# Routing a mixture of experts in four batches between the output projections

## The chip, the cores and the metric

One core of one Trainium2 chip runs the whole program. The metric is device time in microseconds of one execution, from the start to the end of the program on that core. Lower is better. TensorE (PE) multiplies matrices, VectorE (DVE), ScalarE (ACT) and GpSimd (POOL) work on tiles in on-chip memory, SyncE (SP) issues most transfers. Each engine runs its own instructions in order and waits on semaphores.

## What is computed

One layer of a decoder trunk for 1024 prompt rows and 8 sample rows, 1024 wide: a mixer of linear attention and sliding-window attention, an output projection with a gated residual, a norm, and then a mixture of 16 experts of which each row uses two. The part that the change touches:

```python
def moe(h, router_w, router_b, wg, wu, wd):
    x = h.reshape(-1, D)
    scores = sigmoid(x @ router_w)                       # (rows, 16)
    sel = scores + router_b
    group_score = top_k(sel.reshape(n, 4, 4), 2)[0].sum(-1)
    gmask = one_hot(argmax(group_score), 4)              # best group of four experts
    masked = where(repeat(gmask, 4), sel, -inf)
    _, top_idx = top_k(masked, 2)                        # two experts in it
    top_w = take_along_axis(scores, top_idx); top_w /= top_w.sum(-1, keepdims=True)
    hid = silu(einsum('nd,edf->nef', x, wg)) * einsum('nd,edf->nef', x, wu)
    y = einsum('nef,efd->nd', hid * gate[:, :, None], wd)
```

## The kernel before

The program is written as five instruction streams with hand-placed semaphores, in stages that end with a barrier of all five engines (`stage_end`, L494 to L497: each engine drains, counts up, and waits for the other four). Stage 4 is the one of the change: output projection, norm, routing. Stage 5 is the experts.

Rows are worked on in nine tiles: eight of 128 prompt rows and one of the 8 sample rows, which is the last (`PT` = 8 prompt tiles, `NT` = 9). In stage 4 TensorE runs `project(t)` (L1793: 8 k-steps by two halves of 512 columns, 16 matmuls in 32 records) and `route(t)` (L1804: eight transposes of the normed tile, a wait for ScalarE's copy of them, eight logit products), in the order project 0, project 1, route 0, project 2, route 1, ..., project 8, route 7, route 8 (L1819 to L1823). VectorE follows each projection with gate, residual and norm (L1323 to L1341), between whose steps ScalarE squares, sums and takes the root (L960 to L968); SP loads the x tile for it and stores the normed rows to memory (`h2_rows`, L643 to L652).

When all nine routes are done, ScalarE takes the exponential of all logits (L970, L972), and VectorE works on all 9 x 16 = 144 columns at once: scores, best group, two best experts (L1349 to L1382). TensorE counts with two products against a strict triangle and against ones (L1825, L1826): the rank of each row inside its tile for its expert, and the counts per tile. VectorE adds up the tiles (L1389), turns counts into the number of half tiles of each expert and their starts (L1393 to L1398), and gives each row two slots in one packed list (L1400 to L1408). `route_ok` tells the other engines. GpSimd then writes the row numbers into `slot_token` with 18 indirect scatters, two per tile (L725 to L730), and waits for all of them. VectorE meanwhile writes the table of starts `etab` (L1410 to L1412), the weights of the combination (L1415 to L1420) and the low halves of three quarters of the first expert's weights (`split_piece`, L1422 to L1429). SP has issued those loads behind the last norm (L653 to L655), then a store of zeros to `slot_token` (L658) and the load of the first expert's third matrix.

Behind the barrier GpSimd runs one `gather` per tile of an expert (L737): a load of 128 row numbers from `slot_token`, then an indirect gather of those rows of `h2_rows`. TensorE, ScalarE and VectorE run the experts in loops over `etab`. An expert has one full tile of 128 slots and then half tiles of 64. The results go to `slot_rows`, and a last stage gathers two of them per row by `ids`.

Of the kernel before, what the change touches and what calls it, by code (L numbers as in the profile page):

```python
# [27 lines left out]
U32 = mybir.dt.uint32  # L28
# [4 lines left out]
P = 128  # L33
# [26 lines left out]
X_LOADS = ((NT + 1) // 2, NT // 2)  # L60
GN = S + P - 1
# [17 lines left out]
for _name, _w in (("ident", P), ("ones", P), ("cum_mid", P), ("cum", P), ("cum_rest", P), ("strict", P),  # L79
                  ("blk", HA * DV), ("oh", GN), ("ohs", CK + 1), ("seq8", NB), ("diag8", NB * HD),  # L80
                  ("eprio", NE), ("gprio", NG), ("thr", HALVES), ("before", NE * NE), ("srows", 1), ("tokid", NT),
# [45 lines left out]
def build(nc, x_prompt, x_sample, state_gla, cache_win_k, cache_win_v, c_prompt, c_sample, w_ada, b_ada, norm1_g,  # L127
# [23 lines left out]
    slot_token = nc.dram_tensor("slot_token", [SLOTS + 2 * P, 1], U32, kind="Internal").ap()  # L151
    slot_rows = nc.dram_tensor("slot_rows", [SLOTS, D], F32, kind="Internal").ap()

    with ExitStack() as ctx:
# [5 lines left out]
        ids = ctx.enter_context(nc.sbuf_tensor("ids", [P, 2 * NT + NT + 2], U32))  # L160
# [215 lines left out]
        sqj2 = V(a1, D); a1 += D  # L376

# [16 lines left out]
        zero_i = R(SLOTS // P + 2)  # L394
# [46 lines left out]
        so_ps = sem("so_ps"); osq_ok = sem("osq_ok"); ossq_ok = sem("ossq_ok"); ostd_ok = sem("ostd_ok")  # L441
# [8 lines left out]
        ohb_ok = sem("ohb_ok"); qb_ps = sem("qb_ps"); slog_ok = sem("slog_ok"); sprod = sem("sprod")  # L450
        selfd_ok = sem("selfd_ok"); slT_ps = sem("slT_ps"); smax_ok = sem("smax_ok"); sexp_ok = sem("sexp_ok")
        sp_ok = sem("sp_ok"); spT_ps = sem("spT_ps"); spT_ok = sem("spT_ok"); sov_ps = sem("sov_ps")
        smix_ok = sem("smix_ok"); smask_ok = sem("smask_ok")
# [3 lines left out]
        rexp2 = sem("rexp2"); both_ok = sem("both_ok"); rank_ps = sem("rank_ps"); route_ok = sem("route_ok")  # L457
# [43 lines left out]
        def _(sp):  # L501
# [142 lines left out]
            for t in range(NT):  # L644
                if t >= 2:
                    sp.wait_ge(res_ok, t - 1)
                sp.dma_start(xr[t % 2][0:rows_of(t)], xp[t * P:(t + 1) * P] if t < PT else xs).then_inc(x_in[t % 2], 16)
                if t >= 1:
                    sp.wait_ge(norm_ok, NT + t)
                    sp.dma_start(h2_rows[(t - 1) * P:t * P], h2[(t - 1) % 2]).then_inc(h2_out[(t - 1) % 2], 16)  # L650
            sp.wait_ge(norm_ok, 2 * NT)
            sp.dma_start(h2_rows[S:TOK], h2[PT % 2][0:NB]).then_inc(h2_out[PT % 2], 16)  # L652
# [4 lines left out]
            sp.wait_ge(zero_ok, 2)  # L657
            sp.dma_start(slot_token.rearrange("(p n) a -> p (n a)", p=P), zero_i.bitcast(U32)).then_inc(st_zero, 16)  # L658
# [21 lines left out]
            sp.wait_ge(route_ok, 2)  # L680
# [12 lines left out]
        def _(pool):  # L693
# [23 lines left out]
            stage_end(pool, 3)  # L717
            bc.done(nc.gpsimd.partition_broadcast(bcG1, modrow(G1)[32:33]), wait=False)
# [6 lines left out]
            for t in range(NT):  # L725
                n = rows_of(t)
                for j in range(2):
                    nc.gpsimd.indirect_dma_start(  # L728
                        slot_token, bass.IndirectOffsetOnAxis(ap=ids[0:n, 2 * t + j:2 * t + j + 1], axis=0),
                        ids[0:n, 2 * NT + t:2 * NT + t + 1], None).then_inc(st_out, 16)  # L730
# [4 lines left out]
            pool.wait_ge(route_ok, 2)  # L735

            def gather(t, u):  # L737
                pool.dma_start(gidx[:], slot_token[bass.ds(u * HR, P), :]).then_inc(gi_in, 16)
# [29 lines left out]
        def _(act):  # L768
# [191 lines left out]
            for t in range(NT):  # L960
# [5 lines left out]
                if t >= 1:  # L966
                    act.wait_ge(lr_ps, t)
# [76 lines left out]
        def _(dve):  # L1044
# [278 lines left out]
            for t in range(NT):  # L1323
                n = rows_of(t)
                dve.wait_ge(op_ps, t + 1)
                if t == 0:
                    dve.wait_ge(bc_ok, 6)
# [651 lines left out]
```

## Time and profile before

| | us |
|---|---|
| median of three runs (lowest, highest) | 1471.78 (1471.03, 1472.57) |
| the profiled execution, whole time | 1473.51 |
| its span, first to last instruction | 1471.9 |
| TensorE busy | 1194.3 (81%) |
| VectorE busy | 564.3 (38%) |
| ScalarE busy | 465.3 (32%) |
| GpSimd busy | 96.2 (7%) |
| mean granted TensorE clock, share of full speed | 0.897 |

Stage 4 lies between 771.2 and 986.4 us of the span. How to read the rows further down: a row of the chain or of a timeline begins with its start and its length in us; L with a number is a line of the kernel; out<-in are the program's names with the shapes (128x512 is partitions by elements); x32 is the number of instructions in the row; in square brackets stands how long the engine had been idle and who ended it. An engine's name with a q (POOLq) is its sequencer. One f32 matmul leaves two records.

### The profile page before, as it was taken

How to read it: one execution, taken by the hardware profiler on the slowest of the kernel's cores; microseconds unless marked ns; L12 is line 12 of the kernel's file. 1: busy time of each engine (PE TensorE's matmuls, PEld its weight loads, DVE VectorE, ACT ScalarE, POOL GpSimd, SP SyncE). 2: the span in 40 equal slices, each digit the busy share in tenths (PEclk: the TensorE clock that was granted, in tenths of full speed). 3: DMA queues.
4: the chain of work that ended last, by engine and by line, in shares of the span. 5: the costliest groups of instructions: out<-in, count | busy, mean ns of one | idle time of the engine just before them, and what ended most of it. 6: DMA issues, size and time to landing. Idle time of an engine off the chain costs nothing.

```text
span 1471.9 us, 18511 instructions
## 1 busy us (share of the span) xinstructions
PE 1194.3 (81%) x6985; PEld 640.1 (43%) x6986; DVE 564.3 (38%) x851; ACT 465.3 (32%) x777; POOL 96.2 (7%) x110
## 2 busy tenths in 40 slices
PE   4995985975999999999689999305999999999910
PEld 1232553653556565565344444102455545555400
DVE  3256014325222323324802222522553544445347
ACT  0123013413333333334001111203544544445333
POOL 0000000000000000000000000051000001000022
PEclk9997996985999999999589999656999999999965
DMA  6974001004530312107722111416998888978445
GB/s 231 344 284 154 1 1 43 1 9 132 212 92 8 89 41 60 46 12 197 207 85 86 53 52 41 158 52 221 345 364 278 296 281 317 326 272 301 148 170 189
DMA packets 127706, 228.13 MB, mean 155 GB/s; under 512 B 10588, under 2 KB 49145, under 8 KB 127516
## 3 DMA queue, kind: packets, MB, share of 16 engines
q1 hardware_dynamic: 114748, 195.98, 39.1%
q0 software_dynamic: 7168, 21.06, 4.2%
q10 hardware_dynamic: 5728, 10.23, 1.8%
q8 instruction: 43, 0.70, 0.2%
q14 instruction: 19, 0.16, 0.0%
HBM read 193.45 MB, written 33.79 MB: 154 GB/s over the span
## 4 chain that ended last, share of the span: by engine, by line
PE 63%; DVE 7%; ACT 5%; DMA 4%; issue 2%; SPq 2%; POOL 2%; POOLq 0%; ACTq 0%; DVEq 0%
PE banks L1801 9%; PE banks L1864 8%; PE banks L1536 4%; PE banks L1537 4%; PE banks L1538 4%; PE banks L1837 4%; PE banks L1838 4%; PE banks L1839 4%; PE banks L1874 3%; PE banks L1733 2%; PE banks L1888 2%; PE banks L1652 2%; PE banks L1781 2%; PE banks L1845 2%; POOL slot_token L728 1%
## 5 line engine op out<-in xcount | busy, mean ns | idle before, releaser
L1426 DVE SCALAR_TENSOR_TENSOR arena<-arena 128x2048 f16<-128x2048 f32 x64 | 143.8, 2288 | 126.9 <-ACT arena L977 126.9
L1536 PE MATMUL banks<-arena 128*128 128x384 f16 (+4 forms) x536 | 176.2, 329 | 9.3 <-DVE arena L1105 9.3
L1537 PE MATMUL banks<-arena 128*128 128x384 f16 (+4 forms) x536 | 175.9, 328 | 0.0
L1538 PE MATMUL banks<-arena 128*128 128x384 f16 (+4 forms) x536 | 175.7, 328 | 0.0
L977 ACT ACTIVATE arena<-arena 128x2048 f16<-128x2048 f32 x64 | 118.9, 1911 | 72.4 <-DMA arena<-in_moe_w_up_dram 45.0
L1801 PE MATMUL banks<-arena 128*128 128x512 f32 (+1 forms) x288 | 130.6, 614 | 0.3 <-DVEq L496 0.3
L1864 PE MATMUL banks<-arena 128*128 128x512 f32 x256 | 113.9, 598 | 12.5 <-ACT arena L1000 12.5
L1837 PE MATMUL banks<-arena 128*128 128x512 f16 x256 | 98.3, 384 | 2.6 <-DVE arena L1438 2.6
L1838 PE MATMUL banks<-arena 128*128 128x512 f16 x256 | 98.2, 384 | 0.0
L1839 PE MATMUL banks<-arena 128*128 128x512 f16 x256 | 98.0, 383 | 0.0
L1511 PE MATMUL banks<-arena 128*33 128x512 f32 x192 | 85.7, 604 | 0.5 <-ACT arena L777 0.5
L1801 PEld LDWEIGHTS banks<-arena 128*128 128x128 f32 (+1 forms) x288 | 52.2, 184 | 72.3 <-issue 71.8
L1864 PEld LDWEIGHTS banks<-arena 128*128 128x128 f32 x256 | 47.3, 190 | 69.7 <-issue 62.3
L908 ACT ACTIVATE arena<-arena 128x128 f32<-128x128 f32 (+7 forms) x96 | 53.4, 557 | 70.9 <-DVE arena L1235 70.9
L1536 PEld LDWEIGHTS banks<-arena 128*128 128x128 f16 (+1 forms) x536 | 51.8, 97 | 48.7 <-issue 15.3
L1845 PE MATMUL banks<-arena 128*128 128x128 f32 x192 | 26.2, 281 | 56.5 <-DMA arena<-h_rows,gidx 56.5
L1538 PEld LDWEIGHTS banks<-arena 128*128 128x128 f16 (+1 forms) x536 | 52.0, 97 | 36.4 <-issue 1.0
L1235 DVE CUSTOM_DVE_ANT_0 arena<-banks,arena 128x128 f32<-128x128 f32 (+7 forms) x96 | 43.7, 492 | 62.5 <-PE banks L1652 59.3
L1537 PEld LDWEIGHTS banks<-arena 128*128 128x128 f16 (+1 forms) x536 | 51.9, 97 | 34.2 <-issue 0.8
L1260 DVE COPY arena<-banks 128x256 f32<-128x256 f32 (+3 forms) x72 | 27.3, 407 | 74.3 <-PE banks L1733 74.0
L1438 DVE TENSOR_TENSOR arena<-banks,arena 128x1024 f16<-128x1024 f32 x24 | 29.4, 1225 | 63.0 <-ACT arena L991 63.0
L1733 PE MATMUL banks<-arena 128*128 128x128 f32 (+3 forms) x276 | 43.4, 277 | 11.3 <-ACT arena L914 6.7
(337 smaller groups left out, 1562.9 us busy)
## 6 DMA issues: line engine op xcount, KB each, us to landing
arena<-in_moe_w_gate_dram SPq DMA_DIRECT2D x32, 1024.0 KB, 5.4
arena<-in_moe_w_up_dram SPq DMA_DIRECT2D x32, 1024.0 KB, 8.7
arena<-in_moe_w_down_dram SPq DMA_DIRECT2D x16, 2048.0 KB, 11.7
arena<-in_w_ada_dram SPq DMA_DIRECT2D x12, 2048.0 KB
arena<-in_w_in_dram SPq DMA_DIRECT2D x18, 512.0 KB, 5.7
arena<-in_x_prompt_dram SPq DMA_DIRECT2D x16, 512.0 KB, 4.8
slot_rows<-arena SPq DMA_DIRECT2D x2, 4096.0 KB, 20.1
slot_rows<-arena ACTq DMA_DIRECT2D x32, 256.0 KB, 7.2
```

Of the source, the lines that this page charges most:

```text
L977: A(w_hi[s][p // 2][:, (p % 2) * PIECE:(p % 2 + 1) * PIECE], stage[p], ACT.Copy, scale=WS).then_inc(phi_ok, 1)
L1426: v.scalar_tensor_tensor(out=w_lo[s][p // 2][:, part], in0=stage[p], scalar=WS, in1=w_hi[s][p // 2][:, part], op0=ALU.mult, op1=ALU.subtra ...
L1511: last = mm(bank(4 + j % 3, 512, 33), csT[:, k], wa[j % 3][:, k], start=(k == 0), stop=(k == KC - 1))
L1536: mm(out, hTh[:, k, tok], wh(k), start=(first and k == ks[0]), stop=False)
L1537: mm(out, hTh[:, k, tok], wl(k), start=False, stop=False)
L1538: done = mm(out, hTl[:, k, tok], wh(k), start=False, stop=(last and k == ks[-1]))
L1733: last = tr(out[0:w, j * P:(j + 1) * P], p[:, o:o + w], ident)
L1801: last = mm(bank(b + h, 512, n), mixT[:, k, t * P:t * P + n], w[:, 512 * h:512 * h + 512], start=(k == 0), stop=(k == KC - 1))
L1837: mm(out, xh[:, k], wh(k), start=(k == 0), stop=False)
L1838: mm(out, xh[:, k], wl(k), start=False, stop=False)
L1839: done = mm(out, xl[:, k], wh(k), start=False, stop=(k == ks[-1]))
L1864: last = mm(bank(5 + h), hidT[:, k * P:(k + 1) * P], wD[s][:, k * D + h * 512:k * D + h * 512 + 512], start=(k == 0), stop=(k == 3))
```

## The change

The samples' tile is projected first instead of last, in four column groups of TensorE: product k goes to the 32 output partitions from 32*(k % 4) on, so that each group sums two of the eight k-steps; ScalarE copies the four partial sums, and a product with `sel8` (ones at rows r, r + 32, r + 64, r + 96) adds them. Routing is cut in four batches: the samples, tiles 0 to 2, 3 to 5, 6 and 7. Each batch is gated (`gates`, ScalarE), chosen (`choose`, VectorE), counted (`count`, TensorE), and placed (`place`, VectorE) between the projections and norms of later tiles. `run` holds the running counts, so that a rank is final when its batch is placed. An expert now owns a fixed region of 1152 slot numbers in `slot_token`, so the scatters of a batch need no expert starts; GpSimd issues them batch by batch. The packed slots that the combination needs are made once at the end, behind the expert table. The zeros of `slot_token` (now 145 columns) are cleared and stored at the start of the stage.

```diff
+ORDER = (PT,) + tuple(range(PT))
+BATCHES = ((PT, NT), (0, 3), (3, 6), (6, PT))
+CAP = 1152
...
 SP
             sp.dma_start(rw, router_w.rearrange("(k p) n -> p k n", p=P)).then_inc(vec_in, 16)
+            sp.wait_ge(zero_ok, 2)
+            sp.dma_start(slot_token[0:NE * CAP + P].rearrange("(p n) a -> p (n a)", p=P), zero_i.bitcast(U32)).then_inc(st_zero, 16)
...
-            sp.wait_ge(zero_ok, 2)
-            sp.dma_start(slot_token.rearrange("(p n) a -> p (n a)", p=P), zero_i.bitcast(U32)).then_inc(st_zero, 16)
...
 GpSimd
+            nc.gpsimd.memset(zero_i, 0.0).then_inc(zero_ok, 1)
             bc.done(nc.gpsimd.partition_broadcast(bcG1, modrow(G1)[32:33]), wait=False)
...
-            nc.gpsimd.memset(zero_i, 0.0).then_inc(zero_ok, 1)
             pool.wait_ge(st_zero, 16)
-            pool.wait_ge(route_ok, 1)
-            for t in range(NT):
-                n = rows_of(t)
-                for j in range(2):
+            for b, (t0, t1) in enumerate(BATCHES):
+                pool.wait_ge(slots_ok, b + 1)
+                for t in range(t0, t1):
+                    n = rows_of(t)
+                    for j in range(2):
...
-                gather(start, start + e)
+                gather(start, e * CAP)
                 with pool.If(end - start - 1):
-                    with pool.Fori(start + 1, end) as t:
-                        gather(t, t + e + 1)
+                    with pool.Fori(1, end - start) as j:
+                        gather(start + j, e * CAP + j * HR + HR)
...
 ScalarE
+            act.wait_ge(part_ps, 1)
+            A(opart, banks[:, 2048:2048 + D], ACT.Copy).then_inc(part_ok, 1)
+            def gates(b):
+                t0, t1 = BATCHES[b]
+                act.wait_ge(lr_ps, t1 + 1 if t1 < NT else 1)
...
+                A(sco[0:rows_of(t0), t0 * NE:t1 * NE], src, ACT.Exp, scale=-1.0).then_inc(rexp2, 1)
+            for s, t in enumerate(ORDER):
...
                 A(rs[0:n, t:t + 1], ss[0:n, t:t + 1], ACT.Sqrt, scale=1.0 / D, bias=eps[0:n]).then_inc(rms_ok, 1)
+                if t == PT - 1:
+                    A(V(o_stat, 1), C("one"), ACT.Exp)
...
+                for b, (t0, t1) in enumerate(BATCHES):
+                    if t == t1 - 1:
+                        gates(b)
...
 VectorE
+            lk.done(v.memset(banks[:, 2048:2048 + D], 0.0), wait=False)
+            lk.done(v.tensor_tensor(sel8, ident[:, 0:NB], ident[:, 32:32 + NB], ALU.add))
+            lk.done(v.tensor_tensor(sel8, sel8, ident[:, 64:64 + NB], ALU.add))
+            v.tensor_tensor(sel8, sel8, ident[:, 96:96 + NB], ALU.add).then_inc(sel8_ok, 1)
...
+            def choose(b):
+                dve.wait_ge(rexp2, b + 1)
...
+            def place(b):
+                dve.wait_ge(rank_ps, b + 1)
+                for t in range(t0, t1):
+                    lk.done(v.tensor_tensor(rank[:, c], banks[:, r:r + NE], run, ALU.add))
+                    lk.done(v.tensor_tensor(run, run, banks[:, r + 64:r + 64 + NE], ALU.add))
+                lk.done(v.tensor_tensor(v3(E_(tB)), v3(E_(rank)), C("ecap").unsqueeze(1).broadcast_to([P, m, NE]), ALU.add))
+                for j, one in enumerate((one1, one2)):
+                    lk.done(v.tensor_tensor(E_(tA), E_(tB), E_(one), ALU.mult))
+                    lk.done(v.tensor_reduce(sl[:, :, j:j + 1], v3(E_(tA)), AX_X, ALU.add))
+                v.tensor_copy(ids[:, 3 * NT + 2 * t0:3 * NT + 2 * t1], slotf[:, 2 * t0:2 * t1]).then_inc(slots_ok, 1)
...
+            normed(0); normed(1); choose(0); normed(2); place(0); normed(3); normed(4); choose(1); normed(5); place(1)
+            normed(6); normed(7); choose(2); normed(8); place(2); choose(3); place(3)
...
+            for p in range(3):
+                split_piece(0, 0, p)
...
 TensorE
+            def project_samples():
+                pe.wait_ge(sel8_ok, 1)
+                for h in range(2):
+                    for k in range(KC):
+                        r = 32 * (k % 4)
+                        last = mm(banks[r:r + NB, 2048 + 512 * h:2048 + 512 * h + 512], mixT[:, k, S:TOK], w_of(k, h),
+                                  start=(k < 4), stop=(k >= 4), skip_group_check=True)
+                last.then_inc(part_ps, 1)
+                pe.wait_ge(part_ok, 1)
+                for h in range(2):
+                    last = mm(bank(h, 512, NB), sel8, opart[:, 512 * h:512 * h + 512], start=True, stop=True)
+                last.then_inc(op_ps, 1)
...
+            def count(b):
+                pe.wait_ge(both_ok, b + 1)
+                mm(banks[:, 3584 + P:3584 + P + n], C("strict"), w, start=True, stop=True, skip_group_check=True)
+                mm(banks[:, 3584 + P + 64:3584 + P + 64 + n], C("ones"), w, start=True, stop=True, skip_group_check=True).then_inc(rank_ps, 1)
+            project_samples(); project(1); route(0); project(2); route(1); count(0); project(3); route(2); project(4)
+            route(3); project(5); route(4); count(1); project(6); route(5); project(7); route(6); project(8); route(7)
+            count(2); route(8); count(3)
```

In the new functions s counts the tiles in their new order (0 is the samples), and `project(s)`, `route(s)` and `normed(s)` are the steps of before for tile `ORDER[s]`. Some semaphores of stages 1 and 3 are merged, with no change of order there.

## Rows read from the trace of the kernel before

**Rows 1.** the chain of work that ended last, around the routing: start, length, what

```profile
956.62 0.15 DVE etab L1412
...
982.92 1.93 DMA slot_token<-ids
...
984.87 1.53 POOLq L496
...
989.28 5.74 DMA gidx<-slot_token
```

**Rows 2.** TensorE's timeline in stage 4: start, length, line, operation, [idle before]

```profile
771.21 27.73 PE L1801 MATMUL banks<-arena 128*128 128x512 f32 x64 [0.34 <-DVEq L496]
...
798.78 1.04 PE L1810 MATMUL banks<-arena 128*128 128x128 f32 x8
...
800.93 1.96 PE L1817 MATMUL banks<-arena 128*128 128x16 f32 x16 [1.11 <-ACT arena L968]
...
912.86 15.60 PE L1801 MATMUL banks<-arena 128*8 128x512 f32 x32
```

**Rows 3.** stretches: busy time of PE, PEld, DVE, ACT, POOL; granted clock; DMA; GB/s

```profile
836.00:854.00 18.00, 16.89 (x59) 8.92 (x58) 5.12 (x5) 2.47 (x4) 0.00 (x0) 1.00 0.16 58
...
909.50:928.50 19.00, 17.89 (x53) 5.06 (x52) 4.70 (x5) 2.47 (x4) 0.00 (x0) 0.91 0.07 28
...
933.90:938.20 4.30, 1.61 (x24) 1.40 (x24) 1.52 (x4) 1.80 (x4) 0.00 (x0) 0.51 0.28 81
```

**Rows 4.** the chain in an expert's tile and in the window attention

```profile
1084.97 7.13 PE banks L1864 x16
...
1099.18 3.65 PE banks L1888 x16
...
462.89 0.82 PE banks L1648 x16
```

**Rows 5.** VectorE's timeline: first and last of the four large steps of one norm

```profile
799.04 1.23 DVE L1331 TENSOR_TENSOR arena<-banks,arena 128x1024 f32<-128x1024 f32 x1 [5.62 <-PE banks L1801]
...
804.59 1.23 DVE L1340 TENSOR_TENSOR arena<-arena 128x1024 f32<-128x1024 f32 x1
```

**Rows 6.** VectorE's timeline behind the last route

```profile
938.54 1.05 DVE L1350 RECIPROCAL arena<-arena 128x144 f32<-128x144 f32 x1
...
943.01 0.30 DVE L1372 TENSOR_REDUCE arena<-arena 128x9 f32<-128x144 f32 x1
...
947.39 0.23 DVE L1382 TENSOR_SCALAR arena<-arena 128x16 f32<-128x16 f32 x1
...
949.68 1.66 DVE L1389 TENSOR_TENSOR arena<-arena 128x16 f32<-128x16 f32 x8
...
958.71 6.70 DVE L1426 SCALAR_TENSOR_TENSOR arena<-arena 128x2048 f16<-128x2048 f32 x3
```

**Rows 7.** GpSimd's timeline: scatters 1 to 3 and 5 of 18

```profile
957.26 1.24 POOL L728 DMA_INDIRECT slot_token<-ids  x1 [181.16 <-DVE etab L1412]
...
958.80 3.04 POOL L728 DMA_INDIRECT slot_token<-ids  x1 [0.30 <-issue]
...
962.15 1.88 POOL L728 DMA_INDIRECT slot_token<-ids  x1 [0.30 <-issue]
...
966.54 0.96 POOL L728 DMA_INDIRECT slot_token<-ids  x1 [0.30 <-issue]
```

**Rows 8.** ScalarE's timeline: a copy, a table load, the last of three splits

```profile
799.86 1.02 ACT L968 ACTIVATE arena<-banks 128x1024 f32<-128x1024 f32 x1 [9.21 <-PE banks L1810]
...
936.61 1.28 ACT L970 ACT_TABLE_LOAD   x1
...
946.55 1.91 ACT L977 ACTIVATE arena<-arena 128x2048 f16<-128x2048 f32 x1 [0.79 <-DMA arena<-in_moe_w_up_dram]
```

**Rows 9.** VectorE's groups by form: a clear

```profile
L1108 DVE MEMSET arena<- 128x784 f32 x1 | 0.7, 712 | 0.2 <-DVE arena L1105 0.2
```

**Rows 10.** SP's queue: first load of the first expert

```profile
935.63 0.93 SPq L635 DMA_DIRECT2D arena<-in_moe_w_gate_dram  x2
```

More of the change, by code:

```diff
@@ L393, in build @@
         slotf = R(2 * NT)
-        zero_i = R(SLOTS // P + 2)
+        run = R(NE)
+        sel8 = R(NB)
+        zero_i = R(NE * CAP // P + 1)
         X1 = V(A_X1, NT * D).rearrange("p (t n) -> p t n", t=NT)
@@ L1324, in _, with normed @@
+            lk.done(v.tensor_tensor(sel8, sel8, ident[:, 64:64 + NB], ALU.add))
+            v.tensor_tensor(sel8, sel8, ident[:, 96:96 + NB], ALU.add).then_inc(sel8_ok, 1)
+            lk.done(v.tensor_copy(ids[:, 2 * NT:3 * NT], C("tokid")), wait=False)
+            lk.done(v.memset(run, 0.0))
+            cl.done(v.memset(sco[:, PT * NE:RE], 1.0), wait=False)
+            def normed(s):
+                t = ORDER[s]
                 n = rows_of(t)
-                dve.wait_ge(op_ps, t + 1)
-                if t == 0:
+                dve.wait_ge(op_ps, s + 1)
+                if s == 0:
@@ L1380, in _ @@
-            lk.done(v.tensor_tensor(both, one1, one2, ALU.add))
-            lk.done(v.tensor_scalar(both[:, PT * NE:RE], both[:, PT * NE:RE], C("srows"), None, ALU.mult))
-            nc.vector.sem_inc(both_ok, 1)
-            dve.wait_ge(rank_ps, 1)
-            lk.done(v.tensor_copy(rank, bank(0, RE)), wait=False)
-            lk.done(v.tensor_copy(cnt, bank(1, RE)), wait=False)
-            lk.done(v.memset(base[:, 0:NE], 0.0))
-            for t in range(PT):
-                lk.done(v.tensor_tensor(base[:, (t + 1) * NE:(t + 2) * NE], base[:, t * NE:(t + 1) * NE], cnt[:, t * NE:(t + 1) * NE], ALU.add))
@@ L1392, in _ @@
+            normed(0)
+            normed(1)
+            choose(0)
+            normed(2)
+            place(0)
+            normed(3)
+            normed(4)
+            choose(1)
+            normed(5)
+            place(1)
+            normed(6)
+            normed(7)
+            choose(2)
+            normed(8)
+            place(2)
+            choose(3)
+            place(3)
             c9 = cmp9.rearrange("p (e t) -> p e t", e=NE)
-            lk.done(v.tensor_tensor(c9, bcE(nE, HALVES), C("thr").unsqueeze(1).broadcast_to([P, NE, HALVES]), ALU.is_gt))
+            lk.done(v.tensor_tensor(c9, bcE(run, HALVES), C("thr").unsqueeze(1).broadcast_to([P, NE, HALVES]), ALU.is_gt))
@@ L1805, in route @@
+            def route(s):
+                t = ORDER[s]
                 n = rows_of(t)
[L1806 to L1808 removed]
+                pe.wait_ge(norm_ok, NT + s + 1)
+                if s >= 1:
+                    pe.wait_ge(h2T_ok, s)
                 for k in range(KC):
[L1810 removed]
+                    last = tr(banks[:, 2048 + n * k:2048 + n * k + n], h2[s % 2][0:n, k * P:(k + 1) * P], ident[0:n, 0:n])
@@ L1818, in route @@
                 last.then_inc(lr_ps, 1)
-            project(0)
-            for t in range(NT):
-                if t + 1 < NT:
-                    project(t + 1)
-                route(t)
-            pe.wait_ge(both_ok, 1)
-            mm(bank(0, RE), C("strict"), both, start=True, stop=True)
-            mm(bank(1, RE), C("ones"), both, start=True, stop=True).then_inc(rank_ps, 1)
+            def count(b):
+                t0, t1 = BATCHES[b]
+                pe.wait_ge(both_ok, b + 1)
+                w = both[:, t0 * NE:t1 * NE]
+                n = (t1 - t0) * NE
+                mm(banks[:, 3584 + P:3584 + P + n], C("strict"), w, start=True, stop=True, skip_group_check=True)
+                mm(banks[:, 3584 + P + 64:3584 + P + 64 + n], C("ones"), w, start=True, stop=True, skip_group_check=True).then_inc(rank_ps, 1)
+            project_samples()
+            project(1)
+            route(0)
+            project(2)
+            route(1)
+            count(0)
+            project(3)
+            route(2)
+            project(4)
+            route(3)
+            project(5)
+            route(4)
+            count(1)
+            project(6)
+            route(5)
+            project(7)
+            route(6)
+            project(8)
+            route(7)
+            count(2)
+            route(8)
+            count(3)
             stage_end(pe, 4)
@@ L1944, in shape_constants @@
     put("srows", r < NB)
+    put("ecap", np.tile(CAP * np.arange(NE), (P, 1)))
     put("tokid", np.arange(NT)[None, :] * P + np.arange(P)[:, None])
```

248 lines of the change are left out of this document (129 added, 119 removed).

## The prediction

> **What bounds the kernel now.** Read first the chain of the work that ended last, around the routing [rows 1]. The last output projection (the eight sample rows) ends at 928.47 [rows 2]. Then one line of dependent work runs: VectorE's norm of that tile, its routing, its choice of experts and slots, until 956.77, when the table of expert starts is written; then GpSimd's 18 scatters one after the other from 957.26 [rows 7], the last of them issued at 982.92 and landed at 984.85; then GpSimd's own barrier step until 986.40. Only behind that barrier may the experts' rows be gathered. I call the time from the end of the last projection to the release of the barrier the tail: 986.40 - 928.47 = 57.9 us, in which TensorE does a few microseconds of work.
>
> Second, TensorE's timeline of the stretch before it [rows 2]: back-to-back projections, 13.9 us each at the full clock (27.73 for the first two), each followed by a route of 4.1 us (transposes 1.04, a wait of 1.11 for ScalarE's copy, logits 1.96). TensorE is the bound there. The sample tile has 8 columns of 128 and its projection takes as long as any other; it took 15.60 because of the clock. Third, the clock by stretch [rows 3]: one period of projection and route runs at 1.00 throughout, another at 0.91; three of the nine projections are the slow kind, each 1.7 us longer, after the short work of a route. In the tail the granted clock is 0.51, the lower of its two levels (1.2 GHz). Fourth, VectorE in a projection [rows 5]: one tile's norm takes 6.78 us from the projection's end (799.04 to 805.82), so of a period of 17.9 some 11 are free.
>
> **The change, part by part.** The profiled execution lasted 1473.51 (span 1471.9); the median shown is 1471.78. I sum on the profiled one and take the difference off the median.
>
> *Head.* The samples' projection goes first and in four column groups. Before it VectorE clears two banks and builds sel8, and TensorE waits: clearing 128 x 1024 is at [rows 9]'s rate 0.93 us (bounds 0.5, if it runs at twice that rate, and 1.25, what a pass of that size costs in [rows 5]), plus three small steps of 0.21 each [rows 6]: 1.6 us. Nothing covers it. Then 32 records, which take 13.87 one by one. Two column groups run at once in this kernel: 16 records in 3.65 against 7.13 [rows 4]. With groups of 32 columns (and two row groups) 16 records of 192 columns take 0.82, 51 ns each, where 192 columns alone would need 162 by the 433 ns of 512 (13.87 / 32): 3.2 at once. 13.87 / 3.2 = 4.3, / 4 = 3.5; I take 4.2, bounds 3.5 and 13.9. ScalarE's copy of the partial sums is 1.02 [rows 8], 1.1 with the hops, and the summing product is two matmuls, four records of 0.43: 1.75. Together 8.65 instead of 13.87: -5.2.
>
> The Trainium skill, "TensorEngine Tiling (Array Packing)", Theoretical Speedup, gives up to 4 times for at most 32 columns; but its Key Properties say that a change of the tiling mode drains TensorE. By the first the 32 records would be 3.5, 0.7 less than I take; two drains are in no row that I read, and the 3.2 above already contains the changes of shape around it.
>
> *SP and GpSimd at the head.* GpSimd's clear of the slot table's zeros moves ahead of four broadcasts, and SP's store of it, with the wait for that clear, ahead of the x loads. Both cost about 1 us there; the x of the samples is needed only at 771.2 + 8.65 = 779.9, so I put it at nothing; with no cover it would be 1. SP's wait for the same store near the tail's end goes away, hidden work either way.
>
> *Loop.* Eight full projections remain. Route 0 is now of 8 rows: 2.0 instead of 4.1. Counts 0 and 1 go between a route and a projection: two small products each, 0.6 at full clock (0.3 to 1.4): +1.2. The choices (28 steps for three tiles) and placements (12) of the batches run on VectorE between norms. A step costs 0.195 us and 0.001 per column (0.21 at 16 columns, 0.34 at 144 with the gap [rows 6]), so a choice of 48 columns takes 28 x 0.22 + 0.3 for the reciprocal = 6.5 and a placement 2.9. Behind each choice the next norm is queued on VectorE, and behind TensorE's wait for the choice (its count) the next projection. ScalarE's gate of a batch waits for the logits, and behind it stand the square and root of the next tile, which then also pay one table load of 1.28 [rows 8]: the norm ends 10.0 after its projection instead of 6.8. 10.0 + 6.5 = 16.5 is still below the period of 17.9, and the norm is asked for only at 17.9, the counts at 22: no wait. If that cover were gone, it would be what a choice exceeds 1.4 us for, times three. The slow clock I leave at three projections: bounds 0 and 7, so -5.1 to +6.8. Loop: -2.1 + 1.2 = -0.9.
>
> The Trainium skill, "ScalarE: Activation LUTs", What ACT_TABLE_LOAD costs, speaks against the gates: it puts a switch at 2.66 us, load and drain. The row shows 1.28, ended at 937.89, and VectorE's second step on the gated values starts at 938.54 [rows 6], with a gate and a step between: a drain of 1.4 has no room there. By the page the norm would end 1.4 later, at 11.4, and the choice at the period's end, still no wait of TensorE.
>
> *Tail.* Now from the end of the last projection, a full tile: norm 6.78 [rows 5]; route 4.1 at the full clock, 7.0 if its 3.0 us of TensorE work runs at half, as before's last route did [rows 3]: 7.0; gate 0.3, its table loaded ahead; choice of 32 columns 27 x 0.215 + 0.37 = 6.2 (9.4, the whole present one, is the upper bound); count 1.3; placement of two tiles, 10 steps, 2.2. That is 23.8: the last batch's slots. Then VectorE goes on: nine steps to the expert table, three of them of 256 or 272 columns, 2.6; three splits of the first expert's weights 6.70 [rows 6]; then sixteen steps of slots and weights of the combination, 4.4; then the barrier: 37.5. The splits need their loads: SP issues them after the last norm, at 7.1; now the same three are in and halved by ScalarE 12.8 us after the first issue (935.63 to 948.46 [rows 8, 10]), and half a MB of norm rows stored beside them adds some 1.5 us: 21.5, before 26.4.
>
> GpSimd has only four scatters left behind the last slots, the other fourteen run beside projections or beside the last choice (six x 1.27 = 7.6 from about 9.7, [rows 7]). From 23.8: 0.5, then 1.24, 0.3 and the others at 0.96 to 3.04 with 0.3 between [rows 1, 7]: 5.5 to 11.7, landing 1.93, barrier step 1.53 [rows 1]: 33.3 to 39.5. The upper end is what they cost beside splits on VectorE: 3.04 and two of 1.9 lie in the 6.70 us of the splits [rows 6], later ones are 0.96. I take a first one free and three slowed as there: 37.0. So VectorE, which was done at 965.4 before [rows 6], now ends together with GpSimd: tail 37.5, range 33.5 to 41. Against 57.9: -20.4.
>
> *Behind the barrier* the first gather and the experts' tiles have the same operations, from other addresses: nothing.
>
> Sum: -5.2 - 0.9 - 20.4 = -26.5. 1473.5 - 26.5 = 1447.0 on the profiled time, 1471.8 - 26.5 = 1445.3 on the median.
>
> **The rivals.** (a) GpSimd ends the tail. The rows for it are the slowed scatters [rows 7]; against it, only four are left. If all three take 3.04: 1.5 to 2 us later, 1447. The Trainium skill, "GPSIMD Engine Reference", 1. Specifications, says that GpSimd shares its SBUF interfaces with VectorE, with contention where VectorE's instruction has two SBUF inputs; the splits are such, and 3.04 against 0.96 agrees. (b) The column groups run one after the other, or the clock falls at every projection: +9.4 or +6.8, so 1454 or so. Against the first are both shapes in [rows 4]. (c) The scatters do not leave the tail, because GpSimd is held up while the batches run: 18 x 1.27 + 0.5 + 3.46 behind 23.8 is a tail of 50.6, 1458. Against it: GpSimd has been idle for 181 us when its first scatter starts [rows 7]. (d) It becomes slower than before: VectorE's batches push the norms past the period, and TensorE waits in every batch. A choice may exceed its 6.5 by 1.4 before the next norm slips, that norm may slip 17.9 - 6.8 = 11 before its route comes late, and to lose 26.5 in three batches TensorE must then wait 9 in each: a choice would have to take 28. The whole choice of nine tiles takes 9.4 now (9.1 from its second step, 938.54 to 947.62 [rows 6]), so only something that is not in the rows would do it.
>
> **How the numbers follow.** Forecast 0.68 with its own range 1440 to 1450 (the clock by 5, the tail by 4, the head by 2); (a) 0.13; (b) 0.11; (c) 0.03; (d) 0.03; 0.02 for a loss of the same kind that just cancels the gain. The range reaches to (a) and to most of (b): 1438 to 1455. A measurement of this kernel can tell about 0.2% from no change, 3 us; all but (d) and the last lie beyond: faster 0.95, same 0.02, slower 0.03.
>
> **What would show it.** The samples' records at the stage's start within 5 us and the first full projection from about 780; no wait of TensorE for VectorE between projections; scatters between projections on GpSimd's timeline and four behind the last slots; from the last projection's end to the first gather's index load some 40 us instead of 60.8 [rows 1, 2]; a barrier that waits for VectorE's last steps instead of GpSimd. Wrong would be: a projection that waits for a norm, samples' records at 430 ns apart, scatters in one row behind the last slots, or a longer first gather that takes the gain back.

## The result and the profile after

The changed kernel takes 1446.26 us (median of four runs, 1445.04 to 1447.15) where the kernel before, on the same chip, takes 1471.64 (1471.03 to 1472.57): a ratio of 0.9824, 95% interval 0.981 to 0.9839, 25.4 us less. Forecast were 1445.3 and 26.5 less, so the time lies inside the range. By stretches it is less good than that: the tail is right to 0.3 us, the head gave less than half of what was forecast, and what was only a rival ends the tail.

The profiled execution of the changed kernel took 1445.04, its span 1443.4. I cut every trace at the same five marks: TensorE's last record of stage 3, the start of the first full projection (of the second one before, since the first took the 13.87 that the samples now stand for), the end of the last projection, the release of GpSimd's barrier step, and the first transposes of an expert's rows.

| stretch | before | forecast | after | difference |
|---|---|---|---|---|
| start of the program to the end of stage 3 | 770.9 | 770.9 | 767.5 | -3.4 |
| head, to the first of the remaining projections | 14.2 | 9.0 | 12.2 | -2.0 |
| loop, to the end of the last projection | 143.4 | 142.5 | 143.7 | +0.3 |
| tail, to the release of the barrier | 57.9 | 37.5 | 37.8 | -20.2 |
| to the first transposes of the experts | 19.1 | 19.1 | 17.1 | -2.0 |
| from there to the end | 466.4 | 466.4 | 465.1 | -1.3 |

The forecast's 9.0 is its 8.65 with the 0.34 of idle ahead of it [rows 2]. The first, fifth and sixth stretch have the same work in both kernels. What their 6.7 us are is asked below, with more traces of the kernel before. The three that the change touches give 21.9 in this pair of traces, not 26.5.

*Head.* TensorE's timeline of the changed kernel (start, length, line, operation, [idle before]):

```profile
770.49 6.14 PE L1870 MATMUL banks<-arena 128*8 128x512 f32 x32 [3.01 <-DVE arena L1347]
777.84 1.88 PE L1875 MATMUL banks<-arena 128*8 128x512 f32 x4 [1.21 <-ACT arena L971]
779.65 14.00 PE L1862 MATMUL banks<-arena 128*128 128x512 f32 x32
```

The samples' 32 records take 6.14, not the 27.73 / 2 of one full projection in [rows 2], so the column groups do run together. But TensorE stands still for 3.01 first, and the stretches (busy time of PE, PEld, DVE, ACT, POOL; granted clock; DMA share; GB/s) show what that does:

```profile
767.70:770.50 2.80, 0.01 (x2) 0.04 (x4) 2.35 (x7) 0.00 (x0) 2.69 (x4) 0.69 0.46 68
770.50:775.00 4.50, 4.50 (x24) 0.91 (x28) 0.07 (x1) 0.00 (x0) 2.29 (x2) 0.50 0.37 117
775.00:776.70 1.70, 1.63 (x12) 0.14 (x4) 0.00 (x0) 0.00 (x0) 0.00 (x0) 0.82 0.00 0
```

The granted clock falls while TensorE waits, and the first 4.5 us of the records run at 0.50, the lower level. What it waits for is the clear and three small steps on VectorE:

```profile
768.09 0.91 DVE L1344 MEMSET banks<- 128x1024 f32 x1 [0.37 <-DVEq L502]
768.91 0.15 DVE L1345 TENSOR_TENSOR arena<-arena 128x8 f32<-128x8 f32 x1
769.10 0.17 DVE L1346 TENSOR_TENSOR arena<-arena 128x8 f32<-128x8 f32 x1
769.30 1.04 DVE L1347 TENSOR_TENSOR arena<-arena 128x8 f32<-128x8 f32 x1
```

and GpSimd's timeline beside them:

```profile
768.00 1.30 POOL L728 PARTITION_BROADCAST arena<-arena  x1
769.16 1.30 POOL L729 PARTITION_BROADCAST arena<-arena  x1
```

The clear costs 0.91, as [rows 9] said. The last of three equal steps takes 1.04 instead of 0.17: it begins when the first of these broadcasts ends and ends 0.12 before the second does. It takes 1.04 in all six traces that have the steps there.

*Loop.* In the list of waits TensorE waits for VectorE nowhere between two projections. The chain shows the same two kinds of projection as [rows 2], 13.8 and 15.5 (granted clock 1.00 and 0.90), now four of the slower kind among eight (the first, of 13.93, is left out):

```profile
795.12 13.93 PE banks L1862 x32
813.57 15.38 PE banks L1862 x32
832.90 15.53 PE banks L1862 x32
852.37 13.83 PE banks L1862 x32
870.62 15.50 PE banks L1862 x32
890.06 13.83 PE banks L1862 x32
907.84 15.54 PE banks L1862 x32
```

*Tail.* The chain of the changed kernel, from the last tile's transposes to the barrier; the list answers to [rows 1] and [rows 7]:

```profile
930.22 1.98 PE banks L1885 x8
...
933.30 3.61 PE banks L1895 x16
...
937.24 0.19 DVE arena L1386
...
943.52 0.64 PE banks L1903 x2
...
946.58 0.18 DVE ids L1433
...
947.02 1.03 POOL slot_token L738
...
948.36 0.96 POOL slot_token L738
...
949.63 7.54 POOL slot_token L738
...
957.47 2.13 DMA slot_token<-ids
959.62 1.53 POOLq L502
```

and VectorE beside the scatters:

```profile
949.61 6.67 DVE L1468 SCALAR_TENSOR_TENSOR arena<-arena 128x2048 f16<-128x2048 f32 x3
...
960.38 0.18 DVE L1487 TENSOR_TENSOR arena<-arena 128x18 f32<-128x18 f32 x1
```

Of 18 scatters four are left behind the last slots. Three of these take about 1.0; the third begins 0.02 after the first split and ends at 957.17, 0.89 after the last one. So GpSimd ends the tail at 961.15, and VectorE had its last step done at 960.56.

### The profile page after: what moved, and what is told of

Same layout as the page of the kernel before. It is cut to its first block, busy times and chain, and to the rows that moved or that the text cites. A ratio compares the mean times of both kernels' runs of the same rounds, so it can differ in the third digit from the quotient of the medians.

```text
span 1443.4 us, 18676 instructions
## 1 busy us (share of the span) xinstructions
PE 1190.1 (82%) x7001; PEld 641.1 (44%) x7002; DVE 584.9 (41%) x969; ACT 474.4 (33%) x787; POOL 99.1 (7%) x110
## 4 chain that ended last, share of the span: by engine, by line
PE 64%; DVE 7%; ACT 5%; DMA 4%; issue 2%; SPq 2%; POOL 1%; POOLq 0%; ACTq 0%; DVEq 0%
PE banks L1862 8%; PE banks L1964 8%; PE banks L1594 4%; PE banks L1596 4%; PE banks L1595 4%; PE banks L1937 4%; PE banks L1938 4%; PE banks L1939 4%; PE banks L1974 3%; PE banks L1791 2%; PE banks L1988 2%; PE banks L1710 2%; PE banks L1945 2%; PE banks L1839 2%; PE banks L1762 1%
## 5 line engine op out<-in xcount | busy, mean ns | idle before, releaser
L1964 PE MATMUL banks<-arena 128*128 128x512 f32 x256 | 113.9, 598 | 12.6 <-ACT arena L1021 12.6
L1862 PE MATMUL banks<-arena 128*128 128x512 f32 x256 | 118.5, 623 | 0.0
L1964 PEld LDWEIGHTS banks<-arena 128*128 128x128 f32 x256 | 47.3, 190 | 69.7 <-issue 62.3
L1862 PEld LDWEIGHTS banks<-arena 128*128 128x128 f32 x256 | 50.5, 200 | 62.6 <-issue 62.5
## 6 DMA issues: line engine op xcount, KB each, us to landing
arena<-in_moe_w_down_dram SPq DMA_DIRECT2D x16, 2048.0 KB, 12.4
```

What stands on the lines that cost most here:

```text
L1862: last = mm(bank(b + h), mixT[:, k, t * P:t * P + P], w_of(k, h), start=(k == 0), stop=(k == KC - 1))
L1964: last = mm(bank(5 + h), hidT[:, k * P:(k + 1) * P], wD[s][:, k * D + h * 512:k * D + h * 512 + 512], start=(k == 0), stop=(k == 3))
```

## The experiments

My theory after the comparison: (1) the head was missed because TensorE's wait brings the clock down, so that records and wait both cost more; (2) the loop hides all that VectorE does in it, with several microseconds to spare; (3) the tail is shorter because the scatters left it, and it ends where it does because the splits hold GpSimd. The rivals: the column groups themselves cost what the head lacks; the loop is close to its limit; the tail's gain comes from the shorter choice, with GpSimd's scatters hidden or not. Each ratio is taken against runs of the kernel before on the same chip: 1470.51 (median of seven) for the first four experiments, 1472.01 (17 runs) for the next four. The changed kernel did not run beside the first four, so "below" or "above the changed kernel" there is against its first 1446.26, whose kernel before took 1471.64. Such a difference is good to 1 or 2 us, and the traces decide.

**Clearing and sel8 a stage earlier.** The clear of the banks and sel8 are done in stage 3, ahead of a wait of VectorE. The computation is the same.

```diff
+            lk.done(v.memset(banks[:, 2048:2048 + D], 0.0), wait=False)
+            lk.done(v.tensor_tensor(sel8, ident[:, 0:NB], ident[:, 32:32 + NB], ALU.add))
...
             dve.wait_ge(sov_ps, 1)
...
             stage_end(dve, 3)
-            lk.done(v.memset(banks[:, 2048:2048 + D], 0.0), wait=False)
-            lk.done(v.tensor_tensor(sel8, ident[:, 0:NB], ident[:, 32:32 + NB], ALU.add))
...
```

> The changed kernel with VectorE's clearing of the two banks and its three sel8 steps moved into the stage before, where VectorE waits 27 us for TensorE. In the changed kernel TensorE idles 2.75 us at the start of stage 4, the granted clock falls to half there, and the 32 narrow records take 6.14 us. Theory 1 (the idle start lets the clock fall, four groups run at once): no wait, the records at full clock in 3.5 us, the head 12.0 to 6.8, total 5 us less than the changed kernel, about 1441. Rival (the narrow products themselves bring the clock down): the wait goes, the records stay near 6, the head 12.0 to 9.3, total 2.5 less, about 1443.7. Second rival (the wait is VectorE held by GpSimd's broadcasts and would come back elsewhere): no change, 1446.

Measured: 1444.27 (1443.64 to 1448.24), ratio 0.9828, interval 0.9811 to 0.9845. TensorE's timeline:

```profile
770.45 3.62 PE L1870 MATMUL banks<-arena 128*8 128x512 f32 x32 [0.33 <-DVEq L502]
775.27 1.88 PE L1875 MATMUL banks<-arena 128*8 128x512 f32 x4 [1.20 <-ACT arena L971]
777.09 9.28 PE L1862 MATMUL banks<-arena 128*128 128x512 f32 x21
```

and the stretch of its 32 records, with the columns of the stretches above:

```profile
770.40:774.10 3.70, 3.62 (x32) 0.77 (x32) 0.29 (x3) 0.00 (x0) 3.65 (x4) 1.00 0.34 60
```

Without the wait the clock stays at 1.00, and the 32 records take 3.62 instead of 13.87 one by one: 3.8 at once. The head is 7.0 instead of 12.2, and the three sel8 steps take 0.15, 0.17 and 0.17, with no broadcast beside them. The Trainium skill, "TensorEngine Tiling (Array Packing)", Theoretical Speedup, states up to 4 times for at most 32 columns; the trace agrees to 4%. The median is only 2.0 below the changed kernel's, less than the 5.2 of the head, and by the ratio (0.9828 against 0.9824) there is no gain at all: by the whole time this experiment decides nothing. In its trace stage 3 ends 2.6 later and the stretch behind the barrier is 1.5 longer than in the changed kernel's, both with the same work. That the narrow products themselves bring the clock down, the first rival, falls with the 1.00; what the head's gain is worth in the whole time is seen only where both edits are made together, below.

**The samples in one group.** Still first, but one product after the other, without the clear, sel8, copy and sum. The computation is the same.

```diff
-                        r = 32 * (k % 4)
-                        last = mm(banks[r:r + NB, 2048 + 512 * h:2048 + 512 * h + 512], mixT[:, k, S:TOK], w_of(k, h),
-                                  start=(k < 4), stop=(k >= 4), skip_group_check=True)
+                        last = mm(bank(h, 512, NB), mixT[:, k, S:TOK], w_of(k, h), start=(k == 0), stop=(k == KC - 1))
```

> The changed kernel with the samples projected first but in one group, 32 records one by one, without the clearing, sel8, the copy of partial sums and the summing product. Theory 1 (the column groups as they stand are worth only the 1.9 us by which the head shrank from 13.87 to 12.0): 13.9 and no wait at the start, so 1.9 us slower than the changed kernel, about 1448. Rival (they are worth the 5.2 us that the prediction summed): 5 slower, 1451. Rival (nothing of value, the clock falls later for them: five slow projections of eight against two of eight before): 3 to 5 faster, 1442.

Measured: 1453.16 (1450.0 to 1454.55), ratio 0.9876, interval 0.9859 to 0.9894, 6.9 above the changed kernel. The two traces differ by 7.8: 3.7 in the head, 3.6 up to the end of stage 3, where the work is the same. Its timeline:

```profile
771.39 15.60 PE L1862 MATMUL banks<-arena 128*8 128x512 f32 x32 [0.33 <-DVEq L502]
```

The head is 15.9, so against this trace the column groups give 3.7 as they stand (3.3 to 4.8 over the six traces with the wait), between the 1.9 of theory 1 and the 5.2 of its rival, and 8.9 with the early clear. 1.7 of each is that these 32 records run at the slow clock, 15.60 instead of 13.87. They are worth their copy and sum in either form, and the rival that they are of no value falls.

**The splits behind the barrier.** The three splits of the first expert's weights are moved from ahead of the barrier to behind it. The computation is the same.

```diff
-            for p in range(3):
-                split_piece(0, 0, p)
...
             stage_end(dve, 4)
-            split_piece(0, 0, 3)
+            for p in range(PIECES):
+                split_piece(0, 0, p)
```

> The changed kernel with VectorE's three splits of the first expert's weights moved from before the last barrier to behind it, where VectorE waits for the first gather. Theory 1 (VectorE's 6.7 us of splits stand on the way twice: they hold one scatter on GpSimd for 7.5 us, and they delay VectorE's own barrier step): the four scatters take 1.27 each, the barrier opens 5.5 us earlier, total 5.5 less than the changed kernel, about 1440.5. Rival (only GpSimd's order counts, a scatter takes long wherever it lies, for example because of the loads beside it): the third scatter stays at 7 us, no gain. Rival (the splits behind the barrier hold the loads of the second expert, or GpSimd's first gather, by as much): gain of 0 to 2, and the first transposes start no earlier.

Measured: 1442.85 (1440.69 to 1444.98), ratio 0.9809, interval 0.9792 to 0.9825. The chain behind the last slots:

```profile
950.54 1.03 POOL slot_token L738
...
951.88 0.96 POOL slot_token L738
...
953.15 0.96 POOL slot_token L738
...
954.41 3.50 DMA slot_token<-ids
957.94 1.53 POOLq L502
```

and VectorE's last step ahead of the barrier, in its timeline:

```profile
957.34 0.18 DVE L1484 TENSOR_TENSOR arena<-arena 128x18 f32<-128x18 f32 x1
```

No scatter is held any more; the tail is 32.6 instead of 37.8, while the median is 3.4 below the changed kernel. The splits then lie beside the first expert's gather, and the stretch to the first transposes stays at 17.3 (17.1 before this edit). So it was the splits that held GpSimd, and they have a place where no cost of theirs is seen.

**All scatters after the last slots.** GpSimd waits for the last batch's slots before its first scatter. The computation is the same.

```diff
-                pool.wait_ge(slots_ok, b + 1)
+                pool.wait_ge(slots_ok, len(BATCHES))
```

> The changed kernel with GpSimd waiting for the last batch before it issues the first scatter; everything else as it is. Theory 1 (the gain of the tail is mainly the fourteen scatters that left it): 18 scatters of 1.27 and the splits' hold of some 6.5 behind 946.8 of the trace, so the barrier 961.2 becomes about 980, total 18 to 19 slower than the changed kernel, about 1465. Rival (the gain is the shorter choice and placement, 18 scatters or 4 matter little because VectorE ends the tail anyway): under 8 slower, below 1454.

Measured: 1465.25 (1461.51 to 1466.96), ratio 0.9953, interval 0.9937 to 0.997. GpSimd's timeline, the first three and the last of 18:

```profile
951.58 1.10 POOL L738 DMA_INDIRECT slot_token<-ids  x1 [174.82 <-issue]
952.98 0.86 POOL L738 DMA_INDIRECT slot_token<-ids  x1 [0.30 <-issue]
954.14 6.59 POOL L738 DMA_INDIRECT slot_token<-ids  x1 [0.30 <-issue]
...
978.74 0.96 POOL L738 DMA_INDIRECT slot_token<-ids  x1 [0.30 <-issue]
```

The median is 19.0 above the changed kernel, as theory 1 had it, and the tail is 55.0. Of the 20.2 that the change took off it, 17.2 come from the scatters that left it; the rival that the shorter choice gave the gain falls, 2.9 are left for it. By itself it is worth more: the first scatter starts 24.2 after the last projection instead of 28.8, and the longer hold beside the splits takes 1.5 of that back.

**The changed kernel again**, for a second trace beside the next three.

> The changed kernel itself, as it is, beside the runs below on one chip: what its median and its stretches vary by from one chip and one call to the next. Its first median was 1446.3, its first trace had stage 4 from 767.8 where four others have 770 to 772. Expected: 1446 within 1.5, a tail of 37.8 and a head of 12.0 within 0.5, and stage 4 from 770 to 772.

Measured: 1447.99 (1445.99 to 1452.39). Its head is 11.3 (3.0 of wait, records 5.17), its tail 37.8 with the third scatter at 7.53, so the tail repeats to 0.1; time and head lie just outside what was expected. The loop is 143.6 as well, though its projections differ (three at 15.5 to 16.1 among eight). Here a slow spell, a stretch at the lower clock, lies partly in a route: its logit products take 2.58 instead of 1.96, at a granted clock of 0.72. The mean granted clock of the loop is 0.95 in both traces. So the slow clock moves its place from execution to execution. Its price in the loop stays in all seven traces without a pad, 143.6 to 143.7; the next run shows that it need not.

**A pad behind a choice.** Useless clears of a tile that is overwritten later stand behind the choice of tiles 0 to 2, ahead of the next norm. Meant were 10 us; the trace has 13.35.

```diff
             choose(1)
+            for _ in range(33):
+                lk.done(v.memset(cmp9, 0.0))
             normed(5)
```

> The changed kernel with 33 useless clears of 272 columns on VectorE, some 10 us, behind the choice of the second batch (tiles 0 to 2). Theory 1 (VectorE has slack between norms: the choice may exceed its 6.5 us by 1.4 before the next norm slips, and that norm by 11 before its route is late): no projection waits, 0 within the noise of 1.5. Rival (VectorE is already at its limit there and each microsecond of a batch is paid): 10 slower.

Measured: 1450.06 (1447.16 to 1451.14), 2.1 above the changed kernel beside it, with ranges that overlap. VectorE's timeline:

```profile
866.88 13.35 DVE L1444 MEMSET arena<- 128x272 f32 x33
880.27 1.22 DVE L1361 TENSOR_TENSOR arena<-banks,arena 128x1024 f32<-128x1024 f32 x1
```

TensorE waits for none of it; the loop is 142.0, even 1.6 shorter, with less of the slow clock. So the 2.1 of the medians is not a wait that the pad made. Between the two traces, whose executions are the two medians, the head is 1.4 longer (records 6.53 instead of 5.17), the stretch to the first transposes 1.9 and the rest 0.7; none of it is work of the pad.

**A longer pad**, 81 clears in the same place; meant were 25 us, the trace has 32.95.

> The same with 81 clears, some 25 us. Theory 1: the norm behind the choice ends 25 - 13.4 = 11.6 us after its route could start, TensorE waits that long once, and nothing gives it back: 10 to 13 slower, with one wait of that length before a route in TensorE's timeline. Rival (no slack): 25 slower. Rival (later tiles give it back): under 5.

Measured: 1469.48 (1466.14 to 1475.84), 21.5 above the changed kernel. The one wait of TensorE for a norm in the loop, and the route behind it:

```profile
905.99 1.97 PE L1887 MATMUL banks<-arena 128*128 128x128 f32 x8 [18.18 <-DVE arena L1370]
909.08 3.60 PE L1897 MATMUL banks<-arena 128*128 128x16 f32 x16 [1.11 <-ACT arena L990]
```

32.95 - 18.18 = 14.8: that much VectorE may be late behind this choice before TensorE feels it, here beside a projection of the slow kind. From there every microsecond counts in full, and the route behind the wait runs at a granted clock of 0.50, 2.6 more. Nothing of it is given back later: the loop is 22.7 longer, of which the projections, with one slow spell more, have some 1.7. The time is far above the 10 to 13 of theory 1, but because the pad was 32.95 and not 25: with its cover of 13.4 theory 1 gives a wait of 19.6.

**Early clear and splits behind the barrier together.** The edits of the first and the third experiment.

> Both edits at once: clearing and sel8 in the stage before, and the three splits behind the barrier. They act on different stretches (head 12.0 to 7.05 in the trace of the first alone, tail 37.8 to 32.6 in the trace of the second alone). Theory 1 (the gains are real and add up): 10 us less than the changed kernel, about 1436, tail 32.6, head 7.1. Rival (the first edit moved the median by only 2 because what the head gains is given back in the loop or at the first gather): 5 less, about 1441.

Measured: 1438.64 (1438.16 to 1441.46), ratio 0.978, interval 0.9765 to 0.9795; the changed kernel beside it has 0.9844, interval 0.9827 to 0.9862. TensorE's first records, in its timeline:

```profile
770.59 3.62 PE L1868 MATMUL banks<-arena 128*8 128x512 f32 x32 [0.33 <-DVEq L502]
```

and the end of the tail, in the chain:

```profile
948.43 3.98 DMA slot_token<-ids
952.43 1.53 POOLq L502
```

The head is 7.0 and the tail 33.0, where each edit alone gave 7.0 and 32.6. This is the best version: 9.35 below the changed kernel beside it, of which the traces show 4.2 in the head and 4.7 in the tail, and 33.4 below the kernel before. So the gains add up, and the rival that the head's is given back falls.

**The kernel before, three times more**, for the stretches in which both kernels have the same work.

> The kernel before, unchanged, for a second trace of its stretches. In nine traces of the changed kernel and its variants the time from the barrier to the first tile's transposes is 16.9 to 19.7 (mean 17.9) and from there to the end 464.4 to 466.2 (mean 465.0); the one trace of before has 19.1 and 466.4. Theory 1 (nothing of the change lies behind the barrier, the difference is from execution to execution): 17 to 19.7 and 464.4 to 466.4, with a mean like that of the variants. Rival (the other slot addresses give about 1.2 and 1.4 there): 19.1 and 466.4 again, within 0.3. In both, head 14.2, loop 143.4, tail 57.9, to 0.3.

> As the run before it, a third trace of the kernel before: theory 1 has the two stretches behind the barrier spread over 17 to 19.7 and 464.4 to 466.4, the rival has 19.1 and 466.4 within 0.3 in each.

> As the two runs before it, a fourth trace of the kernel before: theory 1 has the two stretches behind the barrier spread over 17 to 19.7 and 464.4 to 466.4, the rival has 19.1 and 466.4 within 0.3 in each.

Measured: 1471.00, 1471.96 and 1473.51, one run each. Their stretches, with the first trace and the nine of the changed kernel and its variants:

| stretch | before, four traces | changed and variants, nine traces |
|---|---|---|
| to the end of stage 3 | 770.9, 768.4, 771.3, 772.5 | 767.5 to 772.1, mean 770.6 |
| head and loop | 157.6, 159.3, 157.6, 157.6 | not the same work |
| tail | 57.9 in each | not the same work |
| to the first transposes | 19.1, 18.0, 18.1, 18.2 | 16.9 to 19.7, mean 17.9 |
| from there to the end | 466.4, 465.8, 465.4, 465.6 | 464.4 to 466.2, mean 465.0 |

That these stretches lost 6.7 is mostly chance of the two traces: the means differ by 0.2, 0.4 and 0.8, 1.4 together. The rival, that 19.1 and 466.4 come back, falls. One of the three has 1.7 more in head and loop, which was not expected: the first projection of the stage is of the slow kind there. Whether the last 0.8 is real stays open.

## Why the prediction was right, and where it was not

**The tail, -20.4: right, -20.2.** Its steps, forecast and measured: norm 6.78 and 6.82; route 7.0 and 6.7 (at half clock, as taken); gate 0.3 and 0.31; choice 6.2 and 6.24; count 1.3 and 1.14; placement 2.2 and 2.14; together 23.8 and 23.4. Then, on VectorE, table 2.6 and 2.9, splits 6.70 and 6.67, the sixteen steps 4.4 and 4.35: done 37.2 after the last projection, against 37.5. The prices of small steps in [rows 6] carried over to tiles of another width.

**The end of the tail was rival (a).** I took GpSimd to be done at 37.0 with three slowed scatters. Measured is one at 7.54 and the rest free, done at 37.8. That the two are so close is luck. My 37.0 was too high for its own rows: the bounds 5.5 and 11.7 already hold the 0.5 that is added to them, and the last scatter's own time stands beside a landing that counts from that scatter's start (both begin at 982.92). Without the two it is 34.5 to 35.5, clear of VectorE's 37.5, and the longer hold, which I had not foreseen, made up for it. In [rows 7] each scatter beside the splits ended some 0.8 after the split that it met: 3.04, 1.88, 1.90. Here it was held until all three splits were done: 7.54 or 7.53 in the six traces with the splits beside the last batch, 6.59 in the run with late scatters. The third experiment shows that the splits are the cause; why a scatter passes between two splits before and not after is open. That the end of the tail was cheap to move (5.2 us) was not in the prediction.

**The head, -5.2: mis-sized, -2.0.** The step that failed is the term of 8.65, and in it two parts. The wait was 1.6 and is 2.7 from the barrier's release (3.0 of idle with the hop); 0.9 of the difference is the one sel8 step beside GpSimd's second broadcast. The prediction names these broadcasts, but weighs only what they mean for SP and GpSimd, not that VectorE could meet them. That the broadcast holds the step is read from their times; no run moves the broadcasts alone. The records were 4.2 and are 6.14, or 5.17 in the second trace: not for lack of column groups, which give 3.62 where the clock holds, but because the idle of 3 us let the clock fall. I had the clock at half in [rows 3] for the tail and counted it in the tail alone. Copy and sum, 1.1 and 1.75, are 1.21 and 1.88. Six traces with this head have 11.1 to 12.6 (records 5.05 to 6.53), where 9.0 (8.65 and the hop) was forecast.

**The loop, -0.9: +0.3.** Removed work is 2.5 instead of 2.1 and the counts 1.1 instead of 1.2. The slow clock was left at three projections, 5.1; the trace has four at 6.6 in all, inside the bounds given, and that is why the loop gained nothing. No wait, as forecast. The cover was 12.4 (1.4 and 11) and is 14.8 with the long pad, because a slow projection lay beside that choice and put off the next norm. VectorE's idle ahead of that norm, in the changed kernel's first trace (a quick projection) and its second (a slow one):

```profile
866.24 1.22 DVE L1361 TENSOR_TENSOR arena<-banks,arena 128x1024 f32<-128x1024 f32 x1 [1.75 <-PE banks L1862]
870.98 1.23 DVE L1361 TENSOR_TENSOR arena<-banks,arena 128x1024 f32<-128x1024 f32 x1 [3.46 <-PE banks L1862]
```

So the 1.4 was nearly right beside a quick projection. For ScalarE's part the prediction gave two figures; its timeline at the first norm behind a gate:

```profile
853.67 1.28 ACT L984 ACT_TABLE_LOAD   x1
854.97 0.29 ACT L984 ACTIVATE arena<-arena 128x1 f32<-128x1 f32 x1
```

The step behind the table load starts 0.02 after it, and that norm ends 9.6 after its projection (848.43 to 858.03), where 10.0 was forecast. An estimate from the Trainium skill, "ScalarE: Activation LUTs", What ACT_TABLE_LOAD costs, was 11.4; the trace does not show that drain. Rival (d) needed the cover to be used up and then a wait of 9 in each batch. Only the long pad uses it up, in one batch, and pays 18.2 there. Rival (b) falls in both halves: the groups run at once, and four of eight projections are slow, not all. Rival (c) is not what happened; its 50.6 for the tail has a likeness in the run with late scatters, 55.0, of which 5.6 are the held scatter.

**Behind the barrier, 0: right** within the 1.2 (0.4 and 0.8) that the means of 13 traces leave open.

Of the marks named ahead, the first gather's index load comes 40.6 after the last projection (964.02), as forecast, and no projection waits; the samples' records within 5 us and the barrier that waits for VectorE did not come. The first full projection does start at 779.7, but only because stage 3 ended 3.4 earlier in this trace.

On the mean of the traces the three touched stretches are 22.3 shorter than in the first trace of before (head -2.4, loop +0.3, tail -20.2), and 22.7 than in its four. The medians differ by 25.4, in the second comparison by 24.0. So the forecast of 26.5 came closer to the median than its parts deserve: the head was some 3 too good and the loop 1, and the medians lie 1 to 3 lower than the touched stretches explain, which is luck as far as the traces tell.

## What to carry to other kernels

Cut serial work of a slow queue (here 18 scatters) into batches as soon as a batch is final, and put it beside work of another engine; look then at what runs beside the last batch, because two engines that share something can hold each other there. Work that must be done before a stage's first matmul belongs ahead of an earlier wait: an idle of 3.0 us at this stage's start, 0.3 without it, cost 2.7 by itself and 1.4 to 2.9 more by the clock (records of 5.05 to 6.53 instead of 3.62). When long stretches with equal work differ by as much as the effect, take several traces and compare the touched stretches alone.

## What the runs showed of the hardware that I had not expected

- One indirect scatter on GpSimd, 0.96 alone, was held for 7.54 by three back-to-back VectorE steps with two inputs of 2048 columns, and ended 0.89 after the last. Why scatters beside the same three steps got through sooner in the kernel before (3.04, 1.88, 1.90) is open. The Trainium skill, "GPSIMD Engine Reference", 1. Specifications, says that GpSimd shares its interfaces to on-chip memory with VectorE and that instructions with two such inputs contend; the trace agrees, and shows a hold across several instructions.
- The other direction: a VectorE step of 8 columns took 1.04 instead of 0.17 beside a broadcast on GpSimd of 1.30.
- Two executions of the same program had their slow clock in other projections and the same loop to 0.1 us (143.66 and 143.61).
